# Attention of a two-layer diffusion step: which operand of the value products is loaded, and where the softmax is normalised

## The reference, cut to what matters

```python
# A: differential            w = softmax(s1) - lam * softmax(s2);  o = w @ v;  then an RMS norm of o
# B: 2-D neighbourhood       o = softmax(s + bias, masked) @ v
# C: windowed, sink logit    o = exp(s - max) / (sum + exp(sink - max)) @ v
# D: latent attention        o = softmax(s) @ v
gates  = sigmoid(h @ w_gate)
merged = sum_i gates_i * (o_i @ w_branch_i)
x      = x + gate1 * (merged @ w_out)
x      = x + gate2 * expert_choice_ffn(...)      # 16 experts, each layer
```

## Time and profile before

| | |
|---|---|
| median of 3 runs | 2897.68 us (2896.67 to 2897.86) |
| profiled execution, its span | 2897.7 us |
| TensorE busy | 2709.3 us, 93% |
| VectorE busy | 1930.4 us, 67% |
| ScalarE busy | 1555.7 us, 54% |
| GpSimd busy | 459.5 us, 16% |
| DMA | 593.74 MB, mean 205 GB/s |

### The profile page before, as it was taken

The page is one execution under the profiler, slowest core; times in us unless marked ns, Lnnn a source line. Parts: engine busy times, 40 slices in busy tenths (PEclk is TensorE's granted clock), DMA queues, the critical chain, the costliest instruction groups (busy, mean ns, idle before and its releaser), DMA issues.

```text
span 2897.7 us, 40625 instructions
## 1 busy us (share of the span) xinstructions
PE 2709.3 (93%) x13616; PEld 1920.2 (66%) x13616; DVE 1930.4 (67%) x3006; ACT 1555.7 (54%) x2279; POOL 459.5 (16%) x359
## 2 busy tenths in 40 slices
PE   7899999999998999999989999998999799999995
PEld 1487777777774666666658777777777466666663
DVE  7743566435257999999955346653525799999995
ACT  7534444334224777777743444333422377777774
POOL 1030001212211121211103000121122111112111
PEclk9799999999999999999999999999999899999997
DMA  9630112112347999999962111121234599999995
GB/s 371 231 91 30 33 37 65 52 37 73 118 176 272 379 381 378 382 378 380 383 231 87 34 34 37 48 70 37 66 119 150 194 374 385 378 375 376 381 381 188
DMA packets 191183, 593.74 MB, mean 205 GB/s; under 512 B 23628, under 2 KB 33674, under 8 KB 191054
## 3 DMA queue, kind: packets, MB, share of 16 engines
q1 hardware_dynamic: 171646, 527.68, 49.0%
q0 software_dynamic: 19408, 64.37, 7.5%
HBM read 566.73 MB, written 25.23 MB: 204 GB/s over the span
## 4 chain that ended last, share of the span: by engine, by line
PE 80%; DVE 7%; issue 5%; ACT 5%; DMA 3%; POOL 0%; ACTq 0%; SPq 0%; DVEq 0%; POOLq 0%
PE bank L501 22%; PE bank L503 21%; PE bank L502 21%; PE bank L936 4%; PE bank L908 4%; PE bank L926 2%; ACT high L1140 2%; DVE low L1488 1%; DMA ring<-in_w_mod 1%; PE bank L692 1%; DMA U<-x_normed,idx_g 1%; PE bank L762 1%; PE bank L1051 1%; PE bank L1089 1%; DVE sigr L1675 1%
## 5 line engine op out<-in xcount | busy, mean ns | idle before, releaser
L1140 ACT ACTIVATE high<-ring 128x1024 fp32r<-128x1024 f32 (+1 forms) x976 | 1023.1, 1052 | 401.4 <-PE bank L503 371.4
L1888 DVE TENSOR_TENSOR low<-ring,high 128x1024 fp32r<-128x1024 f32 x736 | 880.3, 1220 | 72.8 <-ACT high L1140 70.9
L501 PE MATMUL bank<-high,hT_high 128*128 128x512 f32 (+2 forms) x1280 | 523.2, 409 | 25.2 <-ACT sigr L1235 13.6
L502 PE MATMUL bank<-low,hT_high 128*128 128x512 f32 (+2 forms) x1280 | 487.4, 381 | 0.0
L503 PE MATMUL bank<-high,hT_low 128*128 128x512 f32 (+2 forms) x1280 | 485.7, 379 | 0.0
L501 PE MATMUL bank<-high,xeT_high 128*80 128x512 f32 x1056 | 419.0, 397 | 5.7 <-issue 3.5
L503 PE MATMUL bank<-high,xeT_low 128*80 128x512 f32 x1056 | 416.8, 395 | 0.0
L502 PE MATMUL bank<-low,xeT_high 128*80 128x512 f32 x1056 | 416.6, 395 | 0.0
L1488 DVE TENSOR_TENSOR low<-ring,high 128x1024 fp32r<-128x1024 f32 (+2 forms) x240 | 285.4, 1208 | 121.4 <-ACT high L1140 120.0
L1342 ACT ACTIVATE att<-bank,st 128x640 f32<-128x640 f32 (+3 forms) x200 | 136.5, 683 | 350.5 <-DVE st L1750 255.8
L501 PEld LDWEIGHTS bank<-high,hT_high 128*128 128x128 f32 x1280 | 244.6, 191 | 79.3 <-ACT sigr L1235 18.2
(11 more groups left out here) (253 smaller groups left out, 3384.0 us busy)
## 6 DMA issues: line engine op xcount, KB each, us to landing
ring<-in_w_e_gate SPq DMA_DIRECT2D x256, 512.0 KB, 5.9
ring<-in_w_e_up SPq DMA_DIRECT2D x256, 512.0 KB, 6.9
ring<-in_w_e_down SPq DMA_DIRECT2D x256, 512.0 KB, 6.6
ring<-in_w_mod SPq DMA_DIRECT2D x64, 512.0 KB, 7.6
ring<-in_w_gate SPq DMA_DIRECT2D x64, 512.0 KB, 4.8
ring<-in_w_in SPq DMA_DIRECT2D x24, 512.0 KB, 3.5
U<-in_w_mod SPq DMA_DIRECT2D x20, 512.0 KB, 5.2
ring<-in_w_branch SPq DMA_DIRECT2D x16, 512.0 KB, 4.4
```

Of the source, the lines that this page charges most:

```text
L501: nc.tensor.matmul(out, lhs[0], rhs_high, start=start, stop=False)
L502: nc.tensor.matmul(out, lhs[0], rhs_low, start=False, stop=False)
L1140: A(high[:, HSLOT[g], :, 0:w], ring[:, SLOT[g], :, 0:w], ACT.Copy).then_inc(high_done, 1)
L1888: V.tensor_tensor(low[:, SLOT[ahead], :, :], ring[:, SLOT[ahead], :, :], high[:, HSLOT[ahead], :, :].bitcast(F32), ALU.subtract).then_inc( ...
```

## The change

In branches D, B and C, V is now the loaded operand and the transposed probabilities move. The result comes out transposed, 64 partitions by 128 columns, and two units share one PSUM area: one on partitions 0 to 63, the other on 64 to 127 (`plan_groups`). B and C pair the two heads of a query tile, D the query tiles 0 with 1 and 2 with 3; D's context tile and all of A stay single. The outputs of D, B and C need no `turn_o`: `turn_o_high` and `turn_o_low` read them from SBUF. Since the query is now on the columns, the row sums are applied before the turn, by a new `normalise` on VectorE. In every step `values` moves to the place right behind `scores`; semaphores `o_ev` and `o_full` count groups. `turn` now waits for `o_ev` of every group that ended before its unit, and for `w_ready` in all branches.

```diff
+def plan_groups():
+    groups, i = [], 0
+    while i < N_UNIT:
+        u = UNITS[i]
+        if u["br"] in "BC" or (u["br"] == "D" and u["m"] in (0, 2)):
+            groups.append((i, i + 1))
+        else:
+            groups.append((i,))
+        i += len(groups[-1])
+    return groups
...
                 def turn(ui):
-                    if un["br"] == "A":
-                        pe.wait_ge(w_ready, len(A_UNITS) * l + A_BEFORE[ui] + 1)
-                    else:
-                        pe.wait_ge(p_ready, N_PASS * l + un["passes"][0] + 1)
+                    pe.wait_ge(w_ready, N_UNIT * l + ui + 1)
...
-                    if ui >= 2:
-                        pe.wait_ge(o_ev, N_UNIT * l + ui - 1)
+                    if GROUPS_BEFORE[ui]:
+                        pe.wait_ge(o_ev, N_GROUP * l + GROUPS_BEFORE[ui])
...
-                def values(ui):
-                    pe.wait_ge(t_dve, TAIL_BEFORE[N_UNIT] * l + TAIL_BEFORE[min(ui + 2, N_UNIT)])
...
+                def values(gi):
+                    pe.wait_ge(t_act, N_UNIT * l + last + 1)
+                    pe.wait_ge(t_dve, TAIL_BEFORE[N_UNIT] * l + TAIL_BEFORE[last + 1])
+                    if gi:
+                        pe.wait_ge(o_ev, N_GROUP * l + gi)
+                    for i, kb in enumerate(kbs):
+                        for z, v in enumerate(group):
+                            if un["br"] == "A":
+                                ins = mm(bank(6, P, P + HD), pT, v_src(un, kb), start=first, stop=final)
+                            else:
+                                ins = mm(bank(6, P, 2 * P)[HD * z:HD * (z + 1), :], v_src(un, kb), pT, start=first, stop=final)
...
                 for ui in range(N_UNIT + 2):
                     if ui < N_UNIT:
                         scores(ui)
+                    if ui - 2 in ENDS_AT:
+                        values(ENDS_AT[ui - 2])
                     between(AT[ui][0])
                     if 1 <= ui <= N_UNIT:
                         turn(ui - 1)
                     between(AT[ui][1])
-                    if ui >= 2:
-                        values(ui - 2)
                     between(AT[ui][2])
...
+                def normalise(v):
+                    dve.wait_ge(p_ready, N_PASS * l + p + 1)
+                    if un["br"] == "C":
+                        dve.wait_ge(es_ready, N_C * l + C_BEFORE[v] + 1)
+                        then(V.tensor_tensor(sm[:, p % 8:p % 8 + 1], sm[:, p % 8:p % 8 + 1], es[:, v % 4:v % 4 + 1], ALU.add))
+                    then(V.reciprocal(rinv[:, r:r + 1], sm[:, p % 8:p % 8 + 1]))
+                    V.tensor_scalar(prob[:, p % 4, 0:w], prob[:, p % 4, 0:w], rinv[:, r:r + 1], None, ALU.mult).then_inc(w_ready, 1)
```

More of the change, by code:

```diff
@@ L176, in plan_uses @@
     use, freed, full, at, before, last, open_at = {}, {}, {}, {}, {}, [None, None], None
-    n = {"act": 0, "dve": 0, "full": 0}
+    n, turned = {"act": 0, "dve": 0, "full": 0}, {}
     for x in order:
         if x[0] == "on":
+            continue
+        if x[0] == "oT" and x[1] != "A":
+            n["dve"] += 1
+            turned[x[1:]] = n["dve"]
             continue
@@ L194, in plan_uses @@
         freed[r] = (by, n[by])
+        if x[0] == "oT":
+            turned[x[1:]] = n[by]
         if x[0] == "dense" and x[2] == T - 1:
@@ L208, in plan_uses @@
                 rest.append(c)
-    return use, at, before, freed, full, n, lows, rest
-USE, USE_BANK, BEFORE, FREED, FULL, N_USE, LOWS_AFTER, LOWS_END = plan_uses()
+    return use, at, before, freed, full, n, lows, rest, turned
+USE, USE_BANK, BEFORE, FREED, FULL, N_USE, LOWS_AFTER, LOWS_END, TURNED = plan_uses()
 def count_of(*key):
@@ L943, in turn_o @@
                     bank_free(r)
[L944 to L946 removed]
+                    pe.wait_ge(on_ready, T * l + ms[-1] + 1)
                     for k in range(2):
@@ L958, in between @@
                             prep(*x)
-                        elif what == "oT":
+                        elif what == "oT" and x[0] == "A":
                             turn_o(*x)
@@ L1719, in _ @@
                 for ui in range(N_UNIT + 2):
-                    if ui >= 1 and UNITS[ui - 1:ui] and UNITS[ui - 1]["br"] == "A":
-                        combine(ui - 1)
+                    if 1 <= ui <= N_UNIT:
+                        if UNITS[ui - 1]["br"] == "A":
+                            combine(ui - 1)
+                        else:
+                            normalise(ui - 1)
                     if ui < N_UNIT:
@@ L1755, in _ @@
                             dve.wait_ge(t_full, N_UNIT * l + v + 1)
[L1756 to L1758 removed]
+                            if GROUPS_BEFORE[v]:
+                                dve.wait_ge(o_full, N_GROUP * l + GROUPS_BEFORE[v])
+                            V.tensor_copy(probT[:, P_SLOT[v], 4 * P:5 * P], bank(6, 0, P)).then_inc(t_dve, 1)
                     between(AT[ui][1])
[L1760 to L1771 removed]
                     between(AT[ui][2])
```

98 lines of the change are left out of this document (62 added, 36 removed).

## The result

The changed kernel takes 2905.1 us, the median of 12 runs (2897.7 to 2909.7), against 2897.1 us for the kernel before, also of 12 (2888.3 to 2900.2). The ratio is 1.0029, with a 95% interval of 1.0020 to 1.0038. The forecast was 2866 us, and a gain: both sign and size were wrong, by 39 us. The text ahead of the prediction takes the two as one for the kernel before, an error of 2 us at most.

A forecast was written before the change was run, and what follows sets the result against it. The prediction took TensorE's own time and its waits to bound attention. Its terms, -14.6 - 3.3 - 2.0 - 7.0 + 11 = -15.9 us a layer, -31.8 for both, gave 2866 us from 2897.7; range 2852 to 2880.

The forecast's parts named there:

- The products: Products with V in D, B and C: paired halves overlap on TensorE, together -14.6 us a layer.
- the 1.42 of the sum: A D or B group of five blocks: 0.35 + 1.07 = 1.42 us after, against 2.22 before.
- Rivals 1 and 2: Products: 1, output halves do not overlap, 2914 us, 12%; 2, narrow loads hold up their passes, 2890 us, 9%.
- the turns of O: Output transposes: 30 a layer go, -3.3 us; their waits for the low part go too, -2.0.
- The wait before `values`: TensorE's wait ahead of the product with V: now asks for a copy one step older, -7.0 us a layer.
- The new wait before `turn`: `turn` waits until VectorE empties the result of the group multiplied in the same step: +11 us a layer.
- The bullets on A and D: New wait before `turn` in branches A and D: +6 us in A and +3.5 in D, a layer.
- The bullet on B and C: New wait before `turn` in B and C: maximum already done, slot 0 covers the copy; 1.5 us a layer.
- `normalise`: VectorE's scaling in D, B and C: 0.6 us plus 0.25 each, done before `turn` asks; no charge.
- rival 3: VectorE's answer is late: each group's turn waits 0.5 us longer, 26 us a layer, 2918 us; 3%.
- The clock: Where A begins in layer 0, granted clock 0.62 for 9 us; dip may go (-3 us) or come twice.
- The sum: All terms together: -15.9 us a layer, -31.8 for both, from 2897.7 to 2866 us.

The follow-up runs named there:

- experiment 2: The changed kernel with all blocks of a pair's first unit on one half, then all of the second, instead of alternating; 2925.3 us, 1.0102.
- experiment 4: The kernel before with only the order edited: product with V and its scaled copy moved right behind the scores; 2932.2 us, 1.0107.
- experiment 12: The kernel before with only the scaling ahead of the turn in D, B and C, and a plain copy of the result; 2918.3 us, 1.0072.
- 8: The changed kernel with turn's wait for the emptied result put before the fifth transpose alone; 2876.1 us, 0.9937.
- experiment 11: experiment 4 with the wait for the emptied result before the fifth transpose alone; 2894.3 us, 0.9988.
- experiment 1: The changed kernel with VectorE emptying a group's result ahead of the next unit's maximum instead of behind it; 2903.9 us, 1.0024.
- experiment 5: The changed kernel with the product and VectorE's copy of its result back behind slot 1, and some turned-block copies later; 2873.6 us, 0.9921.
- 9: experiment 5 with the scaling moved from the next step's start to the end of slot 1 of its own step; 2869.5 us, 0.9904.
- 10: The kernel of 8 with the scaling moved to the end of slot 1 of its own step; 2870.4 us, 0.9901.
- 13: experiment 5 with the probabilities of D, B and C multiplied by 1.0 instead of the reciprocal; 2873.5 us, 0.9919.
- experiments 1 to 4: experiment 1, experiment 2, experiment 4, and the changed kernel without scaling by row sums, reciprocal kept (2880.6 us, 0.9939).

## Why the prediction was wrong, point by point

- *The products: right.* A group of five takes 1.24 us to the next line, in pairs of starts over 1.04 us. With 0.09 for the entry and about 0.1 for the slow line behind it, that is the 1.42 of the sum. Rivals 1 and 2 did not come. What the halves give over one after the other is smaller than thought (experiment 2), since that form overlaps a little too.
- *The products and the turns of O together: right.* The sum had -14.6 - 3.3 - 2.0 = -19.9 a layer, -40 in all. The change is +8 in all; take off 31 for the order (experiment 4) and 21 for the scaling (12), and -44 is left for this part. From the kernels with the wait before the fifth transpose (8, 11, 12) it is 0.9937 - 0.9988 - 0.0072, or -36. Here I take the parts as adding up, which no run proves. TensorE's busy time fell by 25.1 us, not by the 36 of the two terms; the lower clock (below) lengthens what is left, so this neither proves nor refutes them.
- *The wait before `values`: right.* The 7.0 us in ten waits are gone.
- *The new wait before `turn`: the step that failed.* The bullets on A and D said +9.5 a layer; 8.0 were measured. The bullet on B and C said 1.5, because "VectorE has done that step's maximum before, since the scores of both heads were there a step earlier". The scores were there, but VectorE's queue is in order. The maximum stands behind the scaling, and the scaling behind the gate product or split of slot 2, which follows TensorE's own product. That made 12.4 us, 3.7 of them for the last result of A. The step also priced only the idle time at the turn. The order's further costs lie elsewhere: in experiment 1 the delay moved to ScalarE's evictions, and the clock falls behind such waits. In all the order costs +31 us, where the terms say +8. And the working took the wait's place as given: experiments 8 and 11 show that 27 to 34 us hang on transposes that needn't wait.
- *`normalise`: the second step that failed.* "No charge" rested on the average of a D step, 5.1 us, in which the turn comes long after the exponential. In D that held: nearly no wait of the turn for L1718 shows there. In B and C it did not (experiment 5). Taking it away, adding it, doubling it and giving it to another engine give 18 to 26, 21, 22 and 11 us. The 0.6 us assumed was about right (0.55 to 0.56 measured); that its cover makes it free was not. Standing earlier it costs 5 to 10 us less (9, 10); with other values it costs the same (13).
- *The rivals.* The nearest to what came is rival 3, VectorE's answer late, at 3%. It was argued away by the very sentence on B and C that failed. Its price, 0.5 us more for each of 52 groups, is 26 us a layer on top of the 11 of the sum. L950's waits to 714 us were 20.4 in all, 9.4 on top, and they sit in 17 places of up to 4.0 us. So its mechanism came; that its 2918 us lies near is in part luck, since it had neither the scaling nor the clock.
- *The clock: named, and put at nothing.* "The dip may go (-3 us) or come twice." The mean granted clock of the two profiled executions is 0.976 before and 0.971 after. As an estimate, what is missing of the clock times the span, over all runs, is 68 us in the kernel before (mean of 17 runs, experiments 1 to 4) and 83 in the change (12 runs): up to 15 us, if TensorE sets the pace whenever its clock is low. They are inside the two terms above, not beside them.
- *The sum*: 31 - 8 = 23 us too little for the order, 21 too little for the scaling, and within some 4 us for the rest. The two terms together are the 39 us of the miss, with 5 over from adding parts up.

GpSimd has a hand in both terms. GpSimd's and VectorE's timeline in C of the changed kernel:

```profile
673.19 2.52 POOL L2205 TENSOR_TENSOR M<-M,sigr 128x512 f32<-128x512 f32 x2 [1.81 <-DVE sigr L1746]
...
674.72 1.21 DVE L1718 TENSOR_SCALAR att<-att,st 128x384 f32<-128x384 f32 x1
...
675.85 0.29 DVE L1822 TENSOR_TENSOR bank<-bank,mask_sw 128x128 f32<-128x128 f32 x1
...
677.33 0.52 PE L950 MATMUL bank<-ident,att 128*128 128x128 f32 x3 [1.67 <-DVE U L1738]
```

A scaling of 384 columns takes 0.42 us elsewhere and 1.21 here; GpSimd's two adds end at 675.71 and it ends at 675.93. All 15 scalings of over 0.75 us, of 120, overlap operations of GpSimd, 14 of them this add; by their usual times the 15 take 12.3 us too long. VectorE's splits with both inputs in SBUF stretch too, from 1.22 to 1.7 us and, in two places, to 2.03, but the gate products that read a bank stay at 0.67 to 0.69. The turn behind waits 1.67 us. The longest wait of the turn, 4.0 us before 613.63, stands behind a split of 1.72 us and a sum of one column of 1.21, in place of 1.22 and 0.16, both beside two of GpSimd's adds: 1.5 of the 4.0 us. The Trainium skill, "GPSIMD Engine Reference", 1. Specifications, says that GpSimd's SBUF interfaces are shared with VectorE, with contention where VectorE uses both ports or has two inputs in SBUF; the row agrees. How much of the 31 and of the 21 us comes this way was not tried.

What makes up the order's 31 us is seen from attention as a whole, first to last scores of each layer, in the kernel before and in experiments 4 and 11 (columns as in the earlier trace rows):

```profile
210.70:709.00 498.30, 469.66 (x2755) 377.40 (x2756) 242.49 (x611) 201.01 (x428) 46.98 (x40) 0.99 0.15 46
1591.60:2092.20 500.60, 471.27 (x2754) 378.46 (x2756) 242.84 (x611) 201.14 (x428) 47.40 (x41) 0.99 0.15 46
```

```profile
211.20:731.10 519.90, 482.41 (x2756) 380.67 (x2756) 245.28 (x611) 206.75 (x428) 45.76 (x40) 0.97 0.15 44
1615.30:2131.40 516.10, 478.64 (x2756) 378.04 (x2756) 245.68 (x611) 206.66 (x428) 46.15 (x40) 0.98 0.15 44
```

```profile
210.50:709.80 499.30, 471.96 (x2756) 374.30 (x2756) 245.07 (x611) 205.07 (x428) 46.83 (x41) 0.99 0.16 46
1589.10:2085.30 496.20, 468.80 (x2756) 372.16 (x2756) 245.34 (x611) 205.03 (x428) 46.64 (x41) 1.00 0.16 46
```

In these profiles attention takes 37.1 us longer in experiment 4 than in the kernel before: TensorE is idle 17.0 us more, and the same products keep it busy 20.1 us longer, at a lower granted clock. Experiment 11 takes both away again, 20.2 and 20.3 us; its profiled run is its fastest, 5 us under its median. So about half of what the order costs is idle time and half is work that runs longer. The missing clock, reckoned as above over all runs, is 79 us in experiment 4 and 65 in 11, against 68 and 69 for the kernel before beside them, so 10 to 14 us of that half are the clock's, as an estimate. That the waits bring the clock down rests on experiment 11, in which both go with one wait, and on places such as 459 us; what else moves the clock was not tried. For the change itself attention grows by 11.0 us: TensorE is busy 20.4 us less and idle 31.4 us more.

## What to carry to other kernels

Before you price a new wait, write down what stands ahead of the answer in the answering engine's in-order queue in that very step, branch by branch, and start from when that engine comes free, not from when its input is ready. An average share of 49% busy says nothing about it. A wait can cost more than its idle time: in experiment 4 the work ran longer by about as much again, in experiment 12 hardly at all. Put a wait in front of the one instruction that needs it; here that alone turned a loss of 0.3% into a gain of 0.6%. And an operation added to the engine that gives the answers is not free because its own result has time: what it pushes back pays for it. Try it on an engine on which less hangs.

## What the hardware showed beyond that

- Two units on two halves of the output partitions start 0.006 us apart, a pair each 0.109 us, though both read the same 128 rows of the array and write one bank. Rival 2 had quoted the Trainium skill, "TensorE: Matmul & The Clock Gate", Part 3, by which a load hides behind a running pass only if its row group differs. Here all loads stand on the same 128 rows. Two loads of 64 columns and two passes of 128 take 0.109 us together, and in experiment 2, on one half, a load and its pass take 0.109 too, so the loads add nothing; the measurement decides.
- A float32 scaling within SBUF takes 0.55 to 0.56 us for 640 columns, 0.42 for 384 and 0.29 for 128, and up to 1.6 beside GpSimd's adds. For 640 columns the prediction had estimated 0.4 to 0.5. The copy from the bank of 128 columns takes 0.29.
- Doing passes in turn on both halves and one half after the other differ by 0.71 us for 20 passes, where twice the pace would give 1.07.
